# Weight sums by accumulating DMA, moved out of one attention stage and spread over five semaphores

## The chip, the cores and the metric

The kernel runs on one core of a Trainium2 chip. The metric is the device time of one execution in microseconds (us); three runs gave 3639.58 to 3647.89, with a median of 3645.61. The five engines are named as in the profile: PE is TensorE (PEld its weight loads), DVE is VectorE, ACT is ScalarE, POOL is GpSimd, SP is SyncE. Each has its own queue and executes it in order; they meet at semaphores.

## The reference, cut to what matters

The program is two blocks of a network one after the other, all in float32, on 512 tokens of width 1024. The first block has two layers, and only these matter here:

```python
for l in range(2):
    h = rms_norm(x, g_mix[l])
    c_q, c_kv, k_r, qkv_b, qkv_c, gate_logits = split(h @ w_in[l])
    y_a = mla_mixer(c_q, c_kv, k_r, ...)        # latent attention, 8 heads, 4 blocks of 128 queries
    y_b = dilated_mixer(rope(q_b), rope(k_b), v_b)   # 3 groups of 4 heads
    y_c = neighbourhood_mixer(q_c, k_c, v_c, rpb[l]) # 8 heads
    merged = g0 * (y_a @ w_pa[l]) + g1 * (y_b @ w_pb[l]) + g2 * (y_c @ w_pc[l])
    x = x + merged @ w_o[l]
    h = rms_norm(x, g_ffn[l])
    x = x + (silu(h @ w1[l]) * (h @ w3[l])) @ w2[l]
```

The second block (retention, a gated recurrence and two more FFNs) is not touched by the change.

## The kernel before, in words

Every matmul is made of three in single-pass precision: each float32 operand is split into a high and a low part, and high times high, high times low and low times high are added. Weights come from one large DRAM array, `wts`, in chunks of 128 x 1024, in the order in which PE uses them. SP loads chunk after chunk into two slots (`s_raw`); ACT rounds a chunk to its high part (`wh`) and DVE subtracts that for the low part (`wl`). The softmax work stands between these splits in the queues of ACT and DVE by a plan of levels.

Each layer goes through the stages mix (first projections), MLA, dilated attention in two passes (`dil`, p = 0 and 1), neighbourhood attention (`nbr`), the output projection, and the FFN.

- In MLA (`tensor_mla`, `vector_mla`, `scalar_mla`, `gpsimd_mla`) there are 32 steps, one for each head and block of queries. In step i PE transposes the probabilities of step i - 3, makes the scores of step i and fills up with projections; DVE takes the minimum of the negated scores; ACT takes exp with a sum; DVE takes the reciprocal (`vector_div`, L1273); POOL multiplies the 128 x 512 probabilities `m_p` by it (`gpsimd_div`, L713). PE's transposes of step i wait for that product. POOL also turns keys and queries (`b_qk`, `m_ql`).
- A dilated pass has 13 iterations; divisions (`b_p`, 128 x 768) stand in the first 8, projections for later stages fill PE's queue. At the end of pass 0 POOL multiplies six tiles `b_qk`, for which DVE waits in its queue.
- The neighbourhood attention has 21 iterations; the first 16 hold two divisions (`c_p`, 128 x 256) each, and some a gate product (`acc`) or a turned bias (`c_nb`).

The FFN computes most of its tiles (16 of 22 in a layer, the S units) by a scheme of Strassen's kind with seven products, which needs sums of blocks of weights. Four halves a, b, c, d of two neighbouring weight chunks (each 128 x 512) are to give a + b, b + c, a + b + c and a + b + c + d. These sums are made without any engine's arithmetic: POOL issues DMAs from DRAM to DRAM, plain ones and ones that add onto what is there, into the array `sums` (128 x 2048 for each unit). `weight_sums` (L2659) is a generator that issues a little at each `next`; `sum_turn` (L2701) is one turn. A unit takes three plain copies in one turn (512 KB and twice 256 KB), two adds of 256 KB in the next, and an add of 256 KB in each of two later turns, where they share the turn with those of another unit. Every turn first makes POOL wait, on the one semaphore `sa`, until the last DMA of the turn before has landed. A layer has 49 turns with work. `gpsimd_mla` takes one at the end of each of its 41 iterations, so 41 of the 49 are in MLA and 8 in dilated pass 0.

In the FFN, SP loads the sums and the raw halves of a unit (`load_s`, L734) once its last add has landed.

Of the kernel before, what the change touches and what calls it, by code (L numbers as in the profile page):

```python
# [8 lines left out]
ALU = mybir.AluOpType  # L9
# [36 lines left out]
for _j in range(4):  # L46
# [14 lines left out]

    "pw", "sc", "pl",

    "rawf", "raw0", "raw1", "raw2", "raw3", "rawb", "rawh", "sa", "cst0", "cst", "idn", "tab", "rct", "kct", "msk", "cb0", "cb1", "dec", "ret", "out", "out2",
) + tuple(f"xi{i}" for i in range(8))


# [651 lines left out]
class Sp(Line):  # L719
# [13 lines left out]

    def load_s(self, n, slot, side, *unit):  # L734

        m, wts, sums = self.m, self.m.A["wts"], s_sums(self.m, unit)
        f, l, i = unit
        self.wait_ge("sa", "S4", *unit)
        if side == "a":
            self.e.dma_start(m.raw[slot][:, 0:512], wts[n][:, 0:512]).then_inc(*self.tell(f"raw{slot}", "x", n, by=16))  # L740
            self.e.dma_start(m.raw[slot][:, 512:1024], sums[:, 1024:1536]).then_inc(*self.tell(f"raw{slot}", n, by=16))
            return
        self.e.dma_start(m.raw[slot][:, 0:512], wts[n][:, 0:512]).then_inc(*self.tell(f"raw{slot}", "x", n, by=16))
        self.e.dma_start(m.raw[slot][:, 512:1024], sums[:, 1536:2048]).then_inc(*self.tell(f"raw{slot}", n, by=16))
        before = (f, l, i - 1) if KINDS[i - 1] == "S" else (f, 0, FF - 1) if l else None
        if before:
            self.wait_ge("wl", self.book.s_at(0, before))
        else:
            self.wait_ge("mm", "acc", f, l, 0, 0)
        self.e.dma_start(m.s_b, sums[:, 0:1024]).then_inc(*self.tell("rawb", *unit, by=16))  # L750
        if before:
            self.wait_ge("wl", self.book.s_at(2, before))
        self.e.dma_start(m.s_h, wts[n][:, 512:1024]).then_inc(*self.tell("rawh", *unit, by=16))

    def weights(self, upto, least=-1):
        while not self.inside and self.loaded <= self.book.needs(max(upto + 2, least)):
# [206 lines left out]
def gpsimd_b(L, n):  # L963
    _, l, p, g, w = n
    x = L.m.b_qk[p][2 * g + w]
    L.wait_ge("ev", "shift", *n)
    L.wait_ge("ev", "b_tab", l)
    L.tt(x, x, L.m.b_rc, ALU.mult).then_inc(*L.tell("pl", *n))
# [178 lines left out]
def gpsimd_mix(L, l):  # L1147
    m = L.m
    gpsimd_stat(L, ("mix", l))
    L.wait_ge("rv", "q", l)  # L1150
    L.rsqrt(m.qcol, m.vtmp[:, 0:8], 8).then_inc(*L.tell("pw", "q", l))
    gpsimd_q(L, l, 0)
    L.sums = weight_sums(L, l)
# [102 lines left out]
def gpsimd_q(L, l, h):  # L1256
    m = L.m
    L.wait_ge("hi", "q", l, h)
    L.tt(m.m_q[h % 2][1], m.m_qf, b32(m.m_q[h % 2][0]), ALU.subtract).then_inc(*L.tell("pl", "ql", l, h))
# [22 lines left out]
def gpsimd_div(L, i, P, *key):  # L1282
    m, c = L.m, i % 8
    L.wait_ge("rc", *key, i)
    L.ts(P, P, m.rd[:, c:c + 1], 1.0, ALU.mult, ALU.mult).then_inc(*L.tell("sc", *key, i))
# [42 lines left out]
def gpsimd_y(L, yf, hi, lo, i, at, *key):  # L1328
    L.wait_ge("hi", "y", *key, i)
    L.tt(part(lo, at), yf, b32(part(hi, at)), ALU.subtract).then_inc(*L.tell("pl", "y", *key, i))  # L1330
# [144 lines left out]
def gpsimd_mla(L, l):  # L1475
    m = L.m
    for i in range(41):
        if i < 32:
            gpsimd_div(L, i, m.m_p[i % 4], "mla", l)
        if i - 1 in B_TURN:  # L1480
            gpsimd_b(L, ("b", l, 0) + B_TURN[i - 1])
        if i % 4 == 1 and i < 29:
            gpsimd_q(L, l, i // 4 + 1)
        if 14 <= i < 38 and i % 8 == 6:
            gpsimd_y(L, m.m_yf, *m.ya, (i - 14) // 8, (i - 14) // 8, "mla", l)
        sum_turn(L)


def sync_mla(L, l):
# [69 lines left out]
def gpsimd_proj(L, l, br, i):  # L1559
    m = L.m  # L1560
    L.wait_ge("ev", "p", l, br, i)
    L.tt(m.acc[i], m.acc[i], m.g[i % 2], ALU.add).then_inc(*L.tell("pl", "acc", l, br, i))
# [61 lines left out]
def at(p, i, back):  # L1624

    return [(FILL_V if p else FILL_B)[g] for g in ENDS[p][i - back]] if i >= back else []
# [240 lines left out]
def gpsimd_dil(L, l, p):  # L1867
    key = ("dil", l, p)
    for i in range(13):
        if 1 - p <= i < 8:  # L1870
            gpsimd_div(L, i, L.m.b_p[i % 2], *key)
        if p == 0:
            if i == 2:
                gpsimd_y(L, L.m.m_yf, *L.m.ya, 3, 3, "mla", l)
            for n in at(p, i, 2):
                gpsimd_b(L, ("b", l, 1) + n)
        sum_turn(L)


def sync_dil(L, l, p):  # L1880
# [91 lines left out]
def at_n(i, back):  # L1972
    return [FILL_N[g] for g in ENDS_N[i - back]] if i >= back else []
# [154 lines left out]
def gpsimd_bias(L, l, h):  # L2128
    nb = L.m.c_nb[h % 2]
    L.wait_ge(f"cb{h % 2}", "bias", l, h)  # L2130
    L.ts(nb, nb, -1.0, 1.0, ALU.mult, ALU.mult).then_inc(*L.tell("pl", "cb", l, h))


def gpsimd_nbr(L, l):
    key = ("nbr", l)
    gpsimd_bias(L, l, 0)
    gpsimd_bias(L, l, 1)
    for it in range(21):
        if it < 16:
            for i in (2 * it, 2 * it + 1):  # L2140
                gpsimd_div(L, i, L.m.c_p[i % 6], *key)
        if it >= 2 and it % 2 == 0 and it < 14:
            gpsimd_bias(L, l, it // 2 + 1)
        for x, n in at_n(it, 1):
            if x == "p":
                gpsimd_proj(L, l, 1, n)
        sum_turn(L)


# [498 lines left out]
def s_units():  # L2648
    return [i for i in range(FF) if KINDS[i] == "S"]


def s_sums(m, unit):

    f, l, i = unit
    units = s_units()
    return m.A["sums"][len(units) * l + units.index(i)]


def weight_sums(L, l):  # L2659

    book, wts, units = L.book, L.m.A["wts"], s_units()
    last = None

    def add(to, x, *key):
        L.e.dma_start(to, x, accum_op=ALU.add).then_inc(*L.tell("sa", *key, by=16))

    def of(k):
        unit = ("f", l, units[k])
        return (unit, s_sums(L.m, unit)) + tuple(book.ring[book.s_at(0, unit)][3:5])

    for k in range(len(units) + 3):
        if k < len(units):
            unit, s, a, b = of(k)
            if last:
                L.wait_ge("sa", *last)
            L.e.dma_start(s[:, 0:1024], wts[a]).then_inc(*L.tell("sa", "c0", *unit, by=16))
            L.e.dma_start(s[:, 1024:1536], wts[a][:, 0:512]).then_inc(*L.tell("sa", "c1", *unit, by=16))
            L.e.dma_start(s[:, 1536:2048], wts[b][:, 512:1024]).then_inc(*L.tell("sa", "c2", *unit, by=16))
            last = ("c2",) + unit
            yield  # L2680
        if 0 < k <= len(units):
            unit, s, a, b = of(k - 1)
            L.wait_ge("sa", *last)
            add(s[:, 0:512], wts[a][:, 512:1024], "S3", *unit)
            add(s[:, 512:1024], wts[b][:, 0:512], "S1", *unit)
            last = ("S1",) + unit
            yield
        if 1 < k:
            L.wait_ge("sa", *last)
            if k <= len(units) + 1:  # L2690
                unit, s, a, b = of(k - 2)
                add(s[:, 1024:1536], s[:, 512:1024], "S2", *unit)
                last = ("S2",) + unit
            if 2 < k:
                unit, s, a, b = of(k - 3)
                add(s[:, 1536:2048], s[:, 1024:1536], "S4", *unit)
                last = ("S4",) + unit
            yield


def sum_turn(L):  # L2701
    next(L.sums, None)
# [1447 lines left out]
def gpsimd_program(L):  # L4150
    gpsimd_start(L)
    for l in range(2):
        gpsimd_mix(L, l)
        gpsimd_mla(L, l)
        gpsimd_dil(L, l, 0)
        gpsimd_dil(L, l, 1)
        gpsimd_nbr(L, l)
        gpsimd_out(L, l)
        gpsimd_ffn1(L, l)
    gpsimd_ret(L)  # L4160
    gpsimd_ffn2(L, 0)
    gpsimd_lru(L)
    gpsimd_ffn2(L, 1)
# [114 lines left out]
    return np.ascontiguousarray(v.reshape(-1, 128).T)  # L4278


def pack(plan, inputs):
    w = np.zeros((len(plan), 128, 1024), np.float32)
    for c, tiles in enumerate(plan):
        for p, d in enumerate(tiles):
            if d is None:
                continue
            name, lead, row, cols = d
            cols = np.asarray(list(cols))
            blk = inputs[name][lead][row:row + 128]
            real = cols >= 0  # L4290
            w[c, :, 128 * p:128 * p + 128][:, real] = blk[:, cols[real]]
    return w


# [42 lines left out]
```

## Time and profile before

| | |
|---|---|
| median of three runs | 3645.61 us |
| profiled execution | 3644.53 us, of which the span is 3642.3 |
| mean granted clock of PE | 0.946 |
| PE busy | 3311.8 us, 91% |
| DVE, ACT, POOL busy | 1934.1, 1412.6, 775.3 us |
| DMA through POOL's queue (software) | 28160 packets, 67.12 MB, 10.7% of 16 engines |
| DMA through SP's queue (hardware) | 102816 packets, 317.93 MB, 26.6% |
| sum DMAs | 128 adds and 96 copies |

Busy time says how much an engine had to do, not that it had to do it just then. In the slices of the span (91 us each) one sees where PE falls below nine tenths and where its clock (PEclk, tenths of full speed) does. The tables by stage give each engine's busy time between two moments, the granted clock, the mean busy share of the 16 DMA engines and what they moved. The waits name, for each engine, what ended its idle time. A busy time of POOL for a DMA is the time of issuing it, not of the transfer.

### The profile page before, as it was taken

The numbers are of one execution on the slowest core, as the hardware profiler recorded it, in microseconds if no ns is written. First come the engines' busy times: TensorE is split into PE (matmuls) and PEld (weight loads), VectorE is DVE, ScalarE is ACT, GpSimd is POOL, SyncE is SP. The second block draws the span as 40 slices with busy tenths as digits, with TensorE's granted clock in tenths as the row PEclk, the third lists the DMA queues.
The fourth block names the chain that finished last, engine by engine and source line by source line (L and its number), as shares of the span: only waits on it lengthen the run. The fifth ranks groups of instructions, "written<-read, shape, count | busy, mean of one in ns | idle before, by whom it ended". The sixth has DMA issues, their size and how long they took to land. (4 is left out here: it accounts for less than half of the span.)

```text
span 3642.3 us, 41452 instructions
## 1 busy us (share of the span) xinstructions
PE 3311.8 (91%) x16588; PEld 2802.6 (77%) x16588; DVE 1934.1 (53%) x2948; ACT 1412.6 (39%) x2175; POOL 775.3 (21%) x722
## 2 busy tenths in 40 slices
PE   8654799999999655599999999999999999999998
PEld 7443688888898544488888898888888888888887
DVE  5332447567474433256757475655464427885433
ACT  5322335345353322235535353333242225863221
POOL 2432313301010343312311010211021102541101
PEclk9776899999999767799999999999999999999999
DMA  4556513225442556622334353222223222223322
GB/s 159 111 104 117 106 64 112 97 87 161 139 151 98 124 104 125 113 82 100 100 99 141 125 163 107 90 73 95 87 87 102 95 98 87 93 87 99 101 96 81
DMA packets 131744, 388.10 MB, mean 107 GB/s; under 512 B 15200, under 2 KB 17760, under 8 KB 131552
## 3 DMA queue, kind: packets, MB, share of 16 engines
q1 hardware_dynamic: 102816, 317.93, 26.6%
q0 software_dynamic: 28160, 67.12, 10.7%
q8 instruction: 131, 2.15, 0.2%
q14 instruction: 61, 0.50, 0.0%
q10 hardware_dynamic: 576, 0.40, 0.0%
HBM read 383.29 MB, written 69.21 MB: 124 GB/s over the span
## 5 line engine op out<-in xcount | busy, mean ns | idle before, releaser
L352 PE MATMUL bank<-zh,wh 128*128 128x512 f32 (+1 forms) x2588 | 957.4, 370 | 6.0 <-ACT zh L611 6.0
L670 DVE TENSOR_TENSOR wl<-s_raw,wh 128x1024 fp32r<-128x1024 f32 (+1 forms) x531 | 660.3, 1248 | 558.3 <-ACT wh L611 557.2
L352 PE MATMUL bank<-zh,wl 128*128 128x512 f32 (+1 forms) x2588 | 949.4, 367 | 5.6 <-DVE wl L670 5.6
L352 PE MATMUL bank<-zl,wh 128*128 128x512 f32 (+1 forms) x2588 | 948.8, 367 | 2.2 <-DVE zl L673 2.1
L611 ACT ACTIVATE wh<-s_raw 128x1024 fp32r<-128x1024 f32 (+1 forms) x531 | 555.4, 1052 | 479.9 <-PE bank L352 407.6
L352 PEld LDWEIGHTS bank<-zh,wl 128*128 128x128 f32 x2588 | 494.3, 191 | 91.5 <-DVE wl L670 11.8
L352 PEld LDWEIGHTS bank<-zh,wh 128*128 128x128 f32 x2588 | 496.8, 192 | 83.1 <-ACT zh L611 6.0
L352 PEld LDWEIGHTS bank<-zl,wh 128*128 128x128 f32 x2588 | 495.6, 191 | 78.6 <-DVE zl L673 3.7
L710 POOL TENSOR_TENSOR f_t<-f_t 128x512 f32<-128x512 f32 x84 | 119.3, 1421 | 880.6 <-DVE f_t L666 880.6
L355 PE MATMUL bank<-ident,m_p 128*128 128x128 f32 x256 | 55.9, 358 | 178.6 <-POOL m_p L713 175.6
L716 POOL TENSOR_TENSOR small<-small 128x1 f32<-128x1 f32 (+3 forms) x35 | 43.0, 1230 | 821.9 <-DVE small L663 821.9
L355 PEld LDWEIGHTS bank<-ident,m_p 128*128 128x128 f32 x256 | 37.0, 181 | 206.0 <-issue 195.5
L1448 DVE TENSOR_REDUCE small<-bank 128x1 f32<-128x512 f32 x64 | 44.1, 689 | 212.3 <-PE bank L352 212.1
L352 PE MATMUL bank<-wh,zh 128*128 128x512 f32 (+2 forms) x384 | 147.0, 383 | 0.0
L352 PE MATMUL bank<-f_mh,wh 128*128 128x512 f32 (+1 forms) x396 | 146.4, 370 | 0.0
L352 PE MATMUL bank<-wh,zl 128*128 128x512 f32 (+2 forms) x384 | 145.6, 379 | 0.0
L352 PE MATMUL bank<-f_mh,wl 128*128 128x512 f32 (+1 forms) x396 | 145.3, 367 | 0.0
L352 PE MATMUL bank<-wl,zh 128*128 128x512 f32 (+2 forms) x384 | 145.3, 378 | 0.0
L352 PE MATMUL bank<-f_ml,wh 128*128 128x512 f32 (+1 forms) x396 | 144.2, 364 | 0.0
L352 PE MATMUL bank<-h_h,wl 128*128 128x512 f32 x352 | 138.7, 394 | 0.0
L352 PE MATMUL bank<-h_l,wh 128*128 128x512 f32 x352 | 138.0, 392 | 0.0
L352 PE MATMUL bank<-h_h,wh 128*128 128x512 f32 x352 | 136.6, 388 | 0.0
(383 smaller groups left out, 6169.3 us busy)
## 6 DMA issues: line engine op xcount, KB each, us to landing
s_raw<-in_wts SPq DMA_DIRECT2D x465, 512.0 KB, 3.3
sums<-in_wts POOLq DMA_DIRECT2D x128, 256.0 KB, 5.3
s_raw<-in_wts SPq DMA_DIRECT2D x66, 256.0 KB, 3.0
sums<-in_wts POOLq DMA_DIRECT2D x32, 512.0 KB, 4.6
sums<-sums POOLq DMA_DIRECT2D x64, 256.0 KB, 5.6
s_raw<-sums SPq DMA_DIRECT2D x64, 256.0 KB, 3.8
s_b<-sums SPq DMA_DIRECT2D x32, 512.0 KB, 3.8
s_h<-in_wts SPq DMA_DIRECT2D x32, 256.0 KB, 2.6
```

The source lines that it names most:

```text
L352: return self.e.matmul(out, l, r, start=start, stop=stop, skip_group_check=inside)
L355: return self.e.transpose(out, in_, self.m.ident)
L611: return self.e.activation(out, in_, ACT.Copy, scale=scale)
L670: return self.e.tensor_tensor(out, src, b32(hi), ALU.subtract)
L710: return self.e.tensor_tensor(out, a, b, op)
L716: return self.e.tensor_tensor(out, v, self.m.negh[:, 0:n], ALU.pow)
L1448: L.e.tensor_reduce(m.mn[:, c:c + 1], m.bank[4 + i % 2], AX.X, ALU.min).then_inc(*L.tell("mn", "mla", l, i))
```

## The change

The order in which the DRAM holds the weights of an S unit changes: the two chunks of a unit are laid side by side, so that a row of 2048 elements (a, b, c, d) is one piece of 8 KB (`pack`, `s_raw_tiles`). `load_s` takes its halves from there. A unit is now one plain copy of 1 MB, one add of 512 KB that makes a + b and b + c together, and two adds of 256 KB: four DMAs, each alone in a turn. The turns run through five semaphores, `sa0` to `sa4`, and each waits only for the last DMA on its own, which is the fifth turn back. `gpsimd_mla` has no `sum_turn` any more; each iteration of the dilated passes and of the neighbourhood attention has two. A layer takes 76 turns (64 with a DMA): 52 in the dilated passes and 24 in the first 12 iterations of the neighbourhood attention.

```diff
@@ load_s @@
-        self.wait_ge("sa", "S4", *unit)
+        self.wait_ge(sums_done(i), "S4", *unit)
+        x, y = (0, 1024) if side == "a" else (1024, 1536)
+        self.e.dma_start(m.raw[slot][:, 0:512], raw[:, x:x + 512])...
+        self.e.dma_start(m.raw[slot][:, 512:1024], sums[:, y:y + 512])...
...
@@ gpsimd_mla @@
-        sum_turn(L)
@@ gpsimd_dil @@
         sum_turn(L)
+        sum_turn(L)
@@ gpsimd_nbr @@
         sum_turn(L)
+        sum_turn(L)
@@ weight_sums @@
+def s_raw_tiles(m, n):
+    return m.A["wts"][n:n + 2].rearrange("c p x -> (c p x)").rearrange("(p x) -> p x", x=2048)
...
+    def dma(turn, to, x, *key, **kw):
+        sem = f"sa{turn % 5}"
+        if sem in last:
+            L.wait_ge(sem, *last[sem])
+        L.e.dma_start(to, x, **kw).then_inc(*L.tell(sem, *key, by=16))
+        last[sem] = key
...
     for k in range(len(units) + 3):
...
+        if k < len(units):
+            unit, s, raw = of(k)
+            dma(4 * k, s, raw, "copy", *unit)
+        yield
+        if 0 <= k - 1 < len(units):
+            unit, s, raw = of(k - 1)
+            dma(4 * k + 1, s[:, 0:1024], raw[:, 512:1536], "S31", *unit, accum_op=ALU.add)
+        yield
+        if 0 <= k - 2 < len(units):
+            unit, s, raw = of(k - 2)
+            dma(4 * k + 2, s[:, 1024:1536], s[:, 0:512], "S2", *unit, accum_op=ALU.add)
+        yield
+        if 0 <= k - 3:
+            unit, s, raw = of(k - 3)
+            dma(4 * k + 3, s[:, 1536:2048], s[:, 1024:1536], "S4", *unit, accum_op=ALU.add)
+        yield
+def sums_done(i):
+    return f"sa{(4 * (s_units().index(i) + 3) + 3) % 5}"
@@ pack @@
+    for c in pairs:
+        w[c:c + 2] = np.concatenate([w[c], w[c + 1]], axis=1).reshape(2, 128, 1024)
```

## Rows read from the trace of the kernel before

**Rows 1.** Page, slices: busy tenths of PE and its clock.

```profile
PE   8654799999999655599999999999999999999998
PEclk9776899999999767799999999999999999999999
```

**Rows 2.** By stage: length; busy (x instructions) of each engine; clock, DMA share, GB/s.

```profile
66.90:290.80 223.90, 135.53 (x501) 106.14 (x499) 77.12 (x145) 66.26 (x130) 92.70 (x120) 0.74 0.58 112
290.80:483.10 192.30, 125.41 (x589) 104.06 (x590) 70.81 (x132) 52.51 (x89) 48.41 (x55) 0.80 0.55 111
483.10:577.40 94.30, 93.53 (x470) 77.06 (x469) 48.75 (x90) 37.06 (x62) 12.54 (x10) 1.00 0.25 81
577.40:640.90 63.50, 63.50 (x338) 53.68 (x337) 57.66 (x125) 43.57 (x91) 31.46 (x31) 1.00 0.31 106
1191.90:1418.00 226.10, 134.66 (x501) 104.51 (x499) 77.02 (x145) 66.59 (x130) 92.89 (x120) 0.73 0.57 111
1418.00:1598.80 180.80, 124.91 (x589) 104.65 (x590) 69.73 (x132) 52.52 (x89) 50.21 (x56) 0.80 0.57 118
```

**Rows 3.** Waits of PE and POOL, whole span: total us, times, longest.

```profile
PE bank L355 <- POOL m_p L713: 175.6, 59, 6.1
PE bank L355 <- POOL b_p L713: 86.1, 7, 39.7
...
POOL m_p L713 <- DVE small L1273: 19.0, 2, 9.7
```

**Rows 4.** POOL in order of time: start, us, engine, line, operation [idle before].

```profile
66.89 0.71 POOL L713 TENSOR_SCALAR m_p<-m_p,small 128x512 f32<-128x512 f32 x1 [9.30 <-DVE small L1273]
...
203.09 1.74 POOL L2665 DMA_DIRECT2D sums<-in_wts  x2 [5.17 <-DMA sums<-in_wts]
204.25 1.31 POOL L713 TENSOR_SCALAR m_p<-m_p,small 128x512 f32<-128x512 f32 x1
...
290.78 0.72 POOL L713 TENSOR_SCALAR m_p<-m_p,small 128x512 f32<-128x512 f32 x1
```

**Rows 5.** DVE in order of time, one MLA step.

```profile
217.22 0.69 DVE L1448 TENSOR_REDUCE small<-bank 128x1 f32<-128x512 f32 x1 [7.41 <-PE bank L352]
...
218.76 0.16 DVE L1273 RECIPROCAL small<-small 128x1 f32<-128x1 f32 x1 [0.25 <-ACT m_p L614]
```

**Rows 6.** By window: a copy alone, then two adds alone, at work.

```profile
340.00:342.00 2.00, 0.00 (x0) 0.00 (x0) 0.00 (x0) 0.00 (x0) 0.00 (x0) 1.00 1.05 301
346.00:348.00 2.00, 0.00 (x0) 0.00 (x0) 0.00 (x0) 0.00 (x0) 0.00 (x0) 0.50 1.02 100
```

**Rows 7.** POOL in order of time: issues of sums.

```profile
295.53 1.74 POOL L2665 DMA_DIRECT2D sums<-in_wts  x2 [4.03 <-DMA sums<-in_wts]
306.12 1.66 POOL L2665 DMA_DIRECT2D sums<-sums  x2 [8.85 <-DMA sums<-in_wts]
...
337.99 0.54 POOL L2676 DMA_DIRECT2D sums<-in_wts  x1 [5.22 <-DMA sums<-sums]
...
344.02 1.70 POOL L2665 DMA_DIRECT2D sums<-in_wts  x2 [4.40 <-DMA sums<-in_wts]
352.66 1.64 POOL L2665 DMA_DIRECT2D sums<-sums  x2 [6.94 <-DMA sums<-in_wts]
...
1232.59 0.84 POOL L2665 DMA_DIRECT2D sums<-sums  x1 [5.74 <-DMA sums<-in_wts]
...
1237.87 0.57 POOL L2676 DMA_DIRECT2D sums<-in_wts  x1 [3.70 <-DMA sums<-sums]
```

**Rows 8.** The FFN by window, and SP's loads of sums: first and last start.

```profile
831.00:1140.00 309.00, 309.00 (x1994) 282.32 (x1995) 190.71 (x283) 139.74 (x197) 24.31 (x18) 1.00 0.45 143
...
L741 SPq DMA_DIRECT2D s_raw<-sums x32: 432/432/1482, 831.2 to 2161.2; - x32
```

**Rows 9.** POOL in order of time: divisions of neighbourhood iterations 0 and 11.

```profile
577.45 0.98 POOL L713 TENSOR_SCALAR c_p<-c_p,small 128x256 f32<-128x256 f32 x2 [25.81 <-DVE small L1273]
...
640.90 1.89 POOL L713 TENSOR_SCALAR c_p<-c_p,small 128x256 f32<-128x256 f32 x2 [1.02 <-DVE small L1273]
```

More of the change, by code:

```diff
@@ L62 @@
     "pw", "sc", "pl",
-    "rawf", "raw0", "raw1", "raw2", "raw3", "rawb", "rawh", "sa", "cst0", "cst", "idn", "tab", "rct", "kct", "msk", "cb0", "cb1", "dec", "ret", "out", "out2",
+    "rawf", "raw0", "raw1", "raw2", "raw3", "rawb", "rawh", "sa0", "sa1", "sa2", "sa3", "sa4", "cst0", "cst", "idn", "tab", "rct", "kct", "msk", "cb0", "cb1", "dec", "ret", "out", "out2",
 ) + tuple(f"xi{i}" for i in range(8))
@@ L734, in load_s @@
     def load_s(self, n, slot, side, *unit):
-        m, wts, sums = self.m, self.m.A["wts"], s_sums(self.m, unit)
+        m, sums = self.m, s_sums(self.m, unit)
+        raw = s_raw_tiles(m, n if side == "a" else n - 1)
         f, l, i = unit
-        self.wait_ge("sa", "S4", *unit)
+        self.wait_ge(sums_done(i), "S4", *unit)
+        x, y = (0, 1024) if side == "a" else (1024, 1536)
+        self.e.dma_start(m.raw[slot][:, 0:512], raw[:, x:x + 512]).then_inc(*self.tell(f"raw{slot}", "x", n, by=16))
+        self.e.dma_start(m.raw[slot][:, 512:1024], sums[:, y:y + 512]).then_inc(*self.tell(f"raw{slot}", n, by=16))
         if side == "a":
-            self.e.dma_start(m.raw[slot][:, 0:512], wts[n][:, 0:512]).then_inc(*self.tell(f"raw{slot}", "x", n, by=16))
-            self.e.dma_start(m.raw[slot][:, 512:1024], sums[:, 1024:1536]).then_inc(*self.tell(f"raw{slot}", n, by=16))
             return
-        self.e.dma_start(m.raw[slot][:, 0:512], wts[n][:, 0:512]).then_inc(*self.tell(f"raw{slot}", "x", n, by=16))
-        self.e.dma_start(m.raw[slot][:, 512:1024], sums[:, 1536:2048]).then_inc(*self.tell(f"raw{slot}", n, by=16))
         before = (f, l, i - 1) if KINDS[i - 1] == "S" else (f, 0, FF - 1) if l else None
@@ L752, in load_s @@
             self.wait_ge("wl", self.book.s_at(2, before))
-        self.e.dma_start(m.s_h, wts[n][:, 512:1024]).then_inc(*self.tell("rawh", *unit, by=16))
+        self.e.dma_start(m.s_h, raw[:, 1536:2048]).then_inc(*self.tell("rawh", *unit, by=16))
     def weights(self, upto, least=-1):
@@ L2656, in s_sums @@
     return m.A["sums"][len(units) * l + units.index(i)]
+def s_raw_tiles(m, n):
+    return m.A["wts"][n:n + 2].rearrange("c p x -> (c p x)").rearrange("(p x) -> p x", x=2048)
 def weight_sums(L, l):
[L2661 to L2665, printed above, removed]
+    book, units = L.book, s_units()
+    last = {}
+    def dma(turn, to, x, *key, **kw):
[4 more added lines that the diff above has]
+        last[sem] = key
@@ L2667, in of @@
     def of(k):
         unit = ("f", l, units[k])
-        return (unit, s_sums(L.m, unit)) + tuple(book.ring[book.s_at(0, unit)][3:5])
+        return unit, s_sums(L.m, unit), s_raw_tiles(L.m, book.ring[book.s_at(0, unit)][3])
     for k in range(len(units) + 3):
         if k < len(units):
[L2673 to L2698, printed above, removed]
+            unit, s, raw = of(k)
@@ L4278, in columns, with pack @@
     return np.ascontiguousarray(v.reshape(-1, 128).T)
-def pack(plan, inputs):
+def pack(plan, pairs, inputs):
     w = np.zeros((len(plan), 128, 1024), np.float32)
@@ L4332 @@
     arrays = {f"in_{n}": v for n, v in d.items()}
-    arrays["in_wts"] = pack(book.plan, a)
+    arrays["in_wts"] = pack(book.plan, sorted({r[3] for r in book.ring if r[0] == "s"}), a)
     r = _run(nc, [arrays], core_ids=[0])
```

## Prediction

> **What bounds the kernel now.** I read the slices of the page first [rows 1]. TensorE (PE) is busy nine tenths and at its full clock nearly everywhere, but in slices 2 to 5 and 14 to 17 it is busy four to seven tenths and its granted clock falls as well. The same stretch comes twice, so it is one stage of each of the two layers. The table by stage [rows 2] gives it edges: latent attention (MLA) from its first to its last division on GpSimd (66.9 to 290.8 and 1191.9 to 1418.0), and from there to the first division of the second dilated pass (290.8 to 483.1 and 1418.0 to 1598.8). PE is busy 135.5 of 223.9 us and 125.4 of 192.3 us, at clocks 0.74 and 0.80. Behind that, in dilated pass 1 and the neighbourhood attention, it is busy 99% or more at 1.00.
>
> The waits say who is late [rows 3]: PE's transposes waited 175.6 us for GpSimd's division of m_p (59 of 64 times) and 86.1 us for that of b_p, while GpSimd waited for its own input of m_p twice. GpSimd's queue is the bound, and not by its arithmetic. Its timeline shows why [rows 4]: each division (about 1 us) stands behind a turn of the weight sums, and each turn starts with idling until the last sum DMA has landed (5.17 us before the one at 203.09, 4.03 before that at 295.53 [rows 7]). 31 steps take 223.9 us, 7.2 us each. The whole kernel's time is thus lost in two places of 416 and 407 us, and the rest doesn't hang on the sums.
>
> **The change part by part.** All against the profiled execution, 3644.5 us (span 3642.3 and 2 us around it); the median of the runs is 1.1 us above it.
>
> *The turn leaves MLA.* 41 turns with their waits and issues go. What is late next? VectorE's step is a chain [rows 5]: the minimum starts at 217.22, then exp on ScalarE, and the reciprocal starts at 218.76 and ends 0.16 later: 1.70 us, of which VectorE idles 0.25 just before the reciprocal. With its 77.1 us of work in 31 steps [rows 2], 2.49 each, and that 0.25, VectorE's step is 2.7 us. ScalarE has 66.3 / 31 = 2.1. PE has 501 matmuls; where it runs without gaps it needs 94.3 / 470 = 0.20 us for each in pass 1 and 63.5 / 338 = 0.19 in the neighbourhood stage [rows 2], so 94 to 100 us, 3.0 to 3.2 us a step, if its clock is full. Three engines that near to each other cost some waiting: I take 3.3 us, 102 us in all. The ends are 2.7 (VectorE's alone) and 6.5 (PE at half its clock: 501 at 0.40). The gain is 223.9 - 102 = 122 and 226.1 - 102 = 124 us.
>
> On the clock: rows 2 show 0.74, between the levels of 1.2 and 2.4 GHz, where PE idles 88 of 224 us, and 1.00 where it does not. The Trainium skill ("TensorE: Matmul & The Clock Gate", Part 1) says the same of the cause: throttled is the default, and activity releases it. It speaks for the full clock once the gaps are gone.
>
> *Eight turns leave the head of dilated pass 0.* There GpSimd, with nothing else to do, works off turn after turn while PE waits for its first b_p: one wait of 39.7 us is in the 86.1. From 290.8 to 483.1 PE has 589 matmuls, 118 us at 0.20. The start of the pass has a chain of its own (turned keys, their low parts, first scores), for which I add 12 us: 130. The gain is 62 and 51 us. The ends: 118 (nothing is exposed), and 160 if half of the present idle time has other causes.
>
> *Two turns in each iteration of the dilated passes and the neighbourhood attention.* 76 turns a layer, 64 of which issue a DMA: 52 in pass 0 and pass 1, 24 in the first 12 iterations of the neighbourhood attention. The bytes are the same 2.1 MB a unit, in 4 DMAs in place of 7. GpSimd's own part: an accumulate occupies it 0.87 us (1.74 for two [rows 4]), a copy about 0.54 [rows 7], so some 3.2 us for two iterations. In the neighbourhood attention GpSimd is busy 31.5 of 63.5 us [rows 2]; 1.6 us on an iteration of 5.8 makes 77%. That alone hides.
>
> The wait for the fifth one back does not stall on latency: it reaches 2.5 iterations back, 14 us at least, and a DMA alone needs 5.3 us from its issue to the next turn [rows 7]. What counts is how much the 16 DMA engines can take. Here two rows speak [rows 6]: a plain copy fills them (share 1.05) and moves 301 GB/s; an accumulate fills them as well (1.02) and moves 100 GB/s. A unit is 1.05 MB copied, 3.5 us, and 1.05 MB accumulated, 10.5 us: 14.0 us of all engines, 3.5 us a turn. The weight loads come on top.
> - Pass 0: 26 turns, 91 us, and about 15 us of weights, in 130 us. Hidden.
> - Pass 1 (94.3 us): 26 turns, 91 us, and 81 GB/s of weights, 7.6 MB at 301 GB/s, 25 us: 116, or 22 too many. Five DMAs in flight lend 17. 5 us are left.
> - Neighbourhood attention, iterations 0 to 11 (first division 577.45, last 640.90, 5.8 us each [rows 9]): 7.0 us of sums and 106 GB/s of weights, 0.61 MB, 2.0 us: 9.0 us. 3.2 us too many, twelve times: 39 us.
> What waits behind a held turn on GpSimd is the next two divisions, the gate products and the turned bias, then PE's transposes, and VectorE, which waits for b_k and the bias in order. PE then has gaps again, and I add 6 us for its clock. Cost: 50 us a layer, 100 in all. Below it could be 0, if accumulates of different units overlap better than two of one unit do; above 75, if engines are only nine tenths full in practice.
>
> That row decides against a rule of the Trainium skill. "DMA: Bandwidth & Descriptors", Anatomy of one DMA, fits a GpSimd DMA as 2.0 us and its bytes at 436 GB/s; an estimate by that page is 4.8 us of movement for a unit in place of 14.0, and then the cost would be nothing and the time 3286. The trace disagrees for accumulates, at 100 GB/s.
>
> *The layout of the pairs, the merged adds, the new addresses in the loads.* Rows of 8 KB in place of 4 KB; the loads of the sum units still take 2 KB a row. They lie beside an FFN in which PE is busy 309.0 of 309 us at 1.00 [rows 8], and are hidden. Landing half a microsecond later would cost nothing there. The sums end in iteration 11 of the neighbourhood attention, some 190 us before the first load of them at 831 [rows 8]: nothing there becomes late. At the worst 5 us.
>
> Sum: 3644.5 - (122 + 124) - (62 + 51) + 100 = 3385.5, about 3386 us.
>
> **The rivals.**
> A. *The DMA engines don't bind.* The cost of 100 is not there: 3286 us. For it: the two rows are of one or two DMAs at a time. Against it: their share is full already.
> B. *MLA's next chain is slower.* PE, VectorE and ScalarE wait for each other, PE's gaps keep its clock between the levels, and a step takes 4.8 us, 149 in all: 94 us less gained, 3480. For it: three loads between 2.1 and 3.2 us with work of 1.2 us in one piece among them. Against it: in the neighbourhood attention VectorE is busy 57.7 of 63.5 us and PE still has no gap [rows 2].
> C. *The turns come one after the other, so slower than before.* If five semaphores buy no overlap, because accumulates get in each other's and the weight loads' way, a unit costs what it costs now: a copy 6.0 us (337.99 to 344.02), the joined add 8.6 (344.02 to 352.66), the two short ones 5.3 each (1232.59 to 1237.87) [rows 7], 25.2 us. Beside weight loads the add took 10.6 (295.53 to 306.12); the whole unit scaled by that is 31 us. 16 units then need 496 us, where pass 0, pass 1 and 12 iterations give 130 + 94 + 64 = 288: 208 us lost a layer, against 180 won. 3644.5 - 359 + 416 = 3702 us. It turns slower above 29.2 us a unit. Against it: nothing in the order holds a turn but the fifth one back.
> D. *A heavier form of my cost*, 75 to 90 us a layer, weights late too: 3435 to 3470.
>
> **How the numbers follow.** My forecast 0.50 (3330 to 3435), A 0.21, B 0.12, D 0.11, C 0.04, and 0.02 for something else that takes all the gain. The range 3295 to 3485 leaves out A's lower end, C and B's upper end. A measurement of this kernel tells 0.2% (7 us) from no change. All cases but C and the last are faster: 0.95; same 0.01; slower 0.04.
>
> **What would show it.** Right: in MLA the steps of m_p about 3.3 us apart, PE's wait for m_p gone to a few us, the clock near 1.00 there; the first wait of PE in pass 0 under 10 us; DMA share near 1 in the neighbourhood attention, GpSimd idle before its sums there on a DMA, and its twelve iterations 8 to 9 us apart in place of 5.8. If these stay at 5.8, A holds; steps of 4.5 us and more in MLA are B; turns 6 to 8 us apart all through are C. The forecast is wrong as a whole if MLA stays near 7 us a step without any sum in it.

## The result, and the profile after

The changed kernel takes 3319.7 us (median of 4 runs, 3317.6 to 3326.3), the kernel before in the same session 3644.3: a ratio of 0.911, 95% interval 0.910 to 0.913. It is 325 us faster; the forecast was 3386, 259 us faster, with 3295 to 3485 as its range. The profiled execution took 3321.6 us, its span 3319.8.

Of the page of the kernel after, the slices (busy tenths of PE, its clock, the DMA engines' share). The two holes in PE's row and in its clock [rows 1] are gone; what is left are eights in slices 5, 6, 16 and 17, where the DMA row shows six to nine:

```profile
PE   9999889999999998899999999999999999999998
PEclk9999989999999999899999999999999999999999
DMA  3176862254431379742345422222232322223232
```

By stage, the kernel after, cut at the same divisions as [rows 2]: length; busy (x instructions) of PE, PEld, DVE, ACT, POOL; clock, DMA share, GB/s:

```profile
67.00:149.30 82.30, 80.81 (x458) 67.52 (x456) 71.02 (x139) 59.95 (x126) 49.73 (x46) 1.00 0.14 46
149.30:284.50 135.20, 124.78 (x632) 104.29 (x633) 73.54 (x138) 55.11 (x94) 37.46 (x38) 0.96 0.62 158
284.50:392.90 108.40, 96.80 (x470) 78.49 (x469) 48.45 (x90) 37.31 (x62) 31.90 (x37) 0.94 0.85 191
392.90:473.10 80.20, 68.46 (x330) 56.18 (x330) 56.82 (x125) 43.49 (x91) 44.70 (x47) 0.89 0.80 182
...
1025.30:1107.60 82.30, 80.86 (x458) 67.48 (x456) 71.02 (x139) 59.96 (x126) 49.74 (x46) 1.00 0.14 45
1107.60:1240.70 133.10, 124.96 (x632) 104.72 (x633) 73.70 (x138) 55.23 (x94) 37.40 (x38) 0.96 0.65 161
1240.70:1347.50 106.80, 96.89 (x469) 78.82 (x469) 48.48 (x90) 37.19 (x62) 31.91 (x37) 0.95 0.85 194
1347.50:1431.10 83.60, 69.46 (x338) 56.51 (x337) 58.10 (x125) 43.45 (x91) 43.70 (x48) 0.92 0.78 175
```

| us, layer 0 / layer 1 | before | forecast | after |
|---|---|---|---|
| MLA | 223.9 / 226.1 | 102 | 82.3 / 82.3 |
| dilated pass 0 | 192.3 / 180.8 | 130 | 135.2 / 133.1 |
| dilated pass 1 | 94.3 / 94.3 | 99 | 108.4 / 106.8 |
| neighbourhood, iterations 0 to 11 | 63.5 / 63.5 | 102 | 80.2 / 83.6 |
| PE's clock | | 6 | in the rows |

MLA and pass 0 give 390 us in both layers together, pass 1 and the first 12 neighbourhood iterations take back 63. PE's waits over the whole span, kernel after (total us, times, longest). GpSimd's m_p and b_p [rows 3] are no longer among them; in their place stand ScalarE's high part of the weights (wh), VectorE's low part (wl) and the low part of c_p:

```profile
PE bank L352 <- ACT wh L611: 31.6, 8, 9.9
PE bank L352 <- DVE wl L670: 17.3, 17, 4.9
PE bank L355 <- DVE c_ptl L670: 12.6, 6, 3.1
```

Why ScalarE is late is to be seen one step further back, in the waits of ScalarE and GpSimd themselves from 149 to 475 us (layer 0), and in one place of the timeline. The waits:

```profile
ACT wh L611 <- DMA s_raw<-in_wts: 66.7, 12, 13.9
...
POOL sums L2674 <- DMA sums<-in_wts: 19.5, 7, 4.2
POOL sums L2674 <- DMA sums<-sums: 10.9, 7, 2.9
```

Rows from 424 to 444 us, in the neighbourhood attention (start, us, engine, line, operation [idle before <- releaser]; here each engine's rows one after the other, first GpSimd's, then SP's queue, then ScalarE):

```profile
425.76 1.41 POOL L2674 DMA_DIRECT2D sums<-in_wts  x2
...
430.29 1.67 POOL L2674 DMA_DIRECT2D sums<-sums  x2
443.04 1.89 POOL L713 TENSOR_SCALAR c_p<-c_p,small 128x256 f32<-128x256 f32 x2 [11.07 <-DVE small L1273]
...
426.31 2.08 SPq L732 DMA_DIRECT2D s_raw<-in_wts  x2
...
441.19 1.06 ACT L611 ACTIVATE wh<-s_raw 128x1024 fp32r<-128x1024 f32 x1 [11.92 <-DMA s_raw<-in_wts]
```

SP issues a weight load at 426.31, between four sum DMAs of GpSimd. ScalarE then stands idle 11.9 us until a weight load has landed (the two issued here took 16.2 us in the median), VectorE and PE behind it, and GpSimd's next division, 11 us later, is held by their work and not by its sums. GpSimd waited only 30 us for sum DMAs in the whole stretch. So the cost of the change is there, but on another road than forecast: not GpSimd held at its turns, but weight loads made late. Its size is measured below (e9).

### The profile page after: what moved, and what is told of

Its sections match the earlier page's. It is cut to its first block, busy times and chain, and to the rows that moved or that the text cites. A ratio compares the mean times of both kernels' runs of the same rounds, so it can differ in the third digit from the quotient of the medians.

```text
span 3319.8 us, 41356 instructions
## 1 busy us (share of the span) xinstructions
PE 3224.9 (97%) x16588; PEld 2739.3 (83%) x16588; DVE 1928.6 (58%) x2948; ACT 1404.8 (42%) x2175; POOL 730.9 (22%) x626
## 3 DMA queue, kind: packets, MB, share of 16 engines
q0 software_dynamic: 14848, 67.12, 10.4%
## 4 chain that ended last, share of the span: by engine, by line
PE 78%; DVE 8%; DMA 6%; ACT 4%; issue 2%; POOL 2%; SPq 0%; ACTq 0%; DVEq 0%; POOLq 0%
PE bank L352 76%; DMA s_raw<-in_wts 5%; DVE wl L670 2%; PE bank L355 2%; ACT wh L611 1%; ACT m_p L614 1%; DVE small L1448 1%; DMA sums<-in_wts 1%; POOL f_t L710 1%; POOL u_g L710 1%; DVE c_kl L670 1%; DVE u_uc L666 0%; DVE m_ptl L670 0%; DVE b_k0l L670 0%; DVE m_qf L660 0%
## 5 line engine op out<-in xcount | busy, mean ns | idle before, releaser
L352 PE MATMUL bank<-zh,wl 128*128 128x512 f32 (+1 forms) x2588 | 949.7, 367 | 15.8 <-DVE wl L670 15.7
L352 PE MATMUL bank<-n_h,wh 128*128 128x256 f32 (+1 forms) x448 | 133.7, 298 | 2.2 <-ACT wh L611 2.2
L352 PE MATMUL bank<-n_h,wl 128*128 128x256 f32 (+1 forms) x448 | 133.2, 297 | 0.9 <-DVE wl L670 0.9
L352 PE MATMUL bank<-n_l,wh 128*128 128x256 f32 (+1 forms) x448 | 133.1, 297 | 0.0
## 6 DMA issues: line engine op xcount, KB each, us to landing
s_raw<-in_wts SPq DMA_DIRECT2D x66, 256.0 KB, 3.1
sums<-sums POOLq DMA_DIRECT2D x64, 256.0 KB, 10.8
s_raw<-sums SPq DMA_DIRECT2D x64, 256.0 KB, 3.7
s_h<-in_wts SPq DMA_DIRECT2D x32, 256.0 KB, 2.6
```

Of the source, the lines that this page charges most:

```text
L352: return self.e.matmul(out, l, r, start=start, stop=stop, skip_group_check=inside)
```

## The experiments

Twelve kernels ran. All times are medians, each with its ratio to the kernel before on the same chip. The stages of layer 0, cut at the same divisions (in the row of e1 and e9 those of e9):

| | us | MLA | pass 0 | pass 1 | nbr. 0 to 11 |
|---|---|---|---|---|---|
| before | 3644 | 223.9 | 192.4 | 94.3 | 63.4 |
| after | 3319.7 | 82.4 | 135.2 | 108.4 | 80.2 |
| e1, e9: no sums | (3499), 3218.8 | 82.4 | 119.4 | 94.3 | 63.0 |
| e11: one row of each sum | 3227.4 | 82.3 | 118.8 | 94.3 | 62.8 |
| e8: plain copies | 3286.3 | 82.4 | 129.8 | 104.0 | 72.9 |
| e7: third one back | 3316.0 | 82.3 | 135.3 | 106.3 | 78.0 |
| e2: last one | 3510.0 | 82.4 | 172.3 | 150.6 | 100.1 |
| e4: old DMAs, new place | 3583.8 | 82.4 | 216.2 | 183.1 | 62.2 |
| e5: new DMAs, old place, last one | 3460.4 | 147.4 | 165.8 | 96.4 | 67.2 |
| e3: new DMAs, old place, fifth one | 3279.9 | 85.5 | 132.2 | 101.3 | 69.2 |
| e6: spread | 3269.0 | 82.4 | 127.6 | 102.3 | 70.4 |
| e12: spread, third one back | 3272.1 | 82.4 | 127.6 | 101.6 | 70.3 |
| e13: spread, more in MLA | 3276.9 | 82.5 | 125.4 | 101.4 | 73.3 |

### What the sums cost: e1, e9, e11, e8

**e1.** The turns do nothing, and the loads of the sum units take the raw weights:

```diff
 def sum_turn(L):
+    return
     next(L.sums, None)
```

> This kernel leaves the weight sums out: no turn issues a DMA and the loads of the S units take raw halves, so its output is not the reference's. It measures what the sums still cost where they now stand. Theory (the sums share the 16 DMA engines with the weight loads, and late loads stop ACT, VectorE and PE): pass 1 falls from 108 to 94 us, the first 12 neighbourhood iterations from 80 to 63.5 us, pass 0 from 135 to about 125 us; in both layers together some 80 us, so 3240 us, and ACT's waits of 6 to 14 us for s_raw go. Rival (the sums are hidden and those waits have another cause): 3300 to 3320 us with the waits still there.

Measured: 3499.1 us (0.959). Both missed, by a slip of mine: the FFN's start on GpSimd still runs the generator to its end, so all 64 sum DMAs of a layer were issued there one behind the other, and PE waited 273.8 us for GpSimd behind them (3 waits, longest 137.9). Its stages before that point are those without sums. The heap at the FFN's start is a measurement of its own: the DMA engines by window, kernel e1, while nothing but sums runs:

```profile
600.00:660.00 60.00, 0.00 (x0) 0.00 (x0) 0.00 (x0) 0.00 (x0) 14.83 (x20) 0.50 1.06 194
```

Full engines (1.06) move 194 GB/s of mixed copies and adds: a unit of 2.1 MB takes 2.1 / 194 = 10.8 us of all 16, not the 14.0 of the forecast.

**e9.** The same, with the generator empty:

```diff
-    for k in range(len(units) + 3):
+    for k in ():
```

> The changed kernel without any sum DMA, also none at the start of the FFN; the loads take the halves of the weights as they are, so the output is not the reference's. Theory (the sums take 47 us a layer in dilated pass 0, pass 1 and the neighbourhood attention, and nothing elsewhere): 3319.7 - 94 = about 3226 us, 3215 to 3240; the stages as in the first run without sums: pass 0 about 119, pass 1 94, neighbourhood iterations 0 to 11 64 us. Rival (the stages lengthened for another reason, or the loads behind are slowed too): above 3250, or below 3210 if the sums also cost something beyond iteration 11.

Measured: 3218.8 us (0.884 [0.883, 0.885]), in the theory's range. The changed kernel is 3319.7 - 3218.8 = 101 us longer, where the forecast had 100 for the sums. Its first three stages behind MLA, to be laid beside those of after:

```profile
149.30:268.80 119.50, 118.95 (x632) 101.61 (x633) 73.73 (x138) 55.34 (x94) 23.47 (x18) 1.00 0.23 76
268.80:363.10 94.30, 93.54 (x470) 77.06 (x469) 48.69 (x90) 37.14 (x63) 12.57 (x11) 1.00 0.24 81
363.10:426.10 63.00, 63.00 (x334) 53.32 (x333) 57.05 (x125) 43.63 (x91) 32.04 (x31) 1.00 0.31 108
```

PE has no gap here, with the clock at 1.00. The differences, 15.7, 14.1 and 17.2 us in layer 0 (14.3, 12.6 and 21.0 in layer 1), make 95 us. The remaining 6 lie outside these stages, and 4.7 of them are not the sums': from the start of PE's last matmul to the end it is 12.3 us in the kernel after, 12.4 in the kernel before and 7.6 in e9. So the sums cost some 96 us. The 95 are gaps and clock: PE's busy time for the same (in the last stage nearly the same) matmuls rose from 118.95 to 124.78, from 93.54 to 96.80 and from 63.0 to 68.5 us, 14.6 of the 47 us of layer 0.

**e11.** Every issue and every wait as they are, but one row of 128 moved:

```diff
-        L.e.dma_start(to, x, **kw)
+        L.e.dma_start(to[0:1], x[0:1], **kw)
```

> The changed kernel with all 64 sum DMAs a layer issued in their places and waited for as they are, but each moves one row of 128 only, and the loads of the sum units take the weights as they are, so the output is not the reference's. Theory (what costs is the time that the sums take of the DMA engines, here under 1% of it): 3219 to 3230 us, as without any sums. Rival (GpSimd's issue of a DMA, some 0.5 to 0.9 us each, or its waits, cost the third that plain copies left over): 3250 to 3290.

Measured: 3227.4 us (0.887 [0.886, 0.888]), the theory. The stages are those without sums to 0.6 us; the 8.6 us above e9 lie after 1335 us, behind the sums of both layers, and 7.8 of them behind the start of PE's last matmul (15.4 us to the end, against 7.6 in e9); why the kernel's end differs between runs is not known. So GpSimd's 64 issues cost nothing in the stages: the bytes do. The waits are not tested by e11, where GpSimd was never idle before a sum DMA; in the changed kernel it waited 30 us for them from 149 to 475 us, and none of PE's waits there names one of its divisions.

**e8.** The same bytes, waits and places, but nothing is added:

```diff
-            dma(4 * k + 1, s[:, 0:1024], raw[:, 512:1536], "S31", *unit, accum_op=ALU.add)
+            dma(4 * k + 1, s[:, 0:1024], raw[:, 512:1536], "S31", *unit)
```

and so for the other two adds.

> The same four DMAs a unit in the same places with the same waits and bytes, but the three adds are plain copies, so the sums are not the reference's. Theory 1 (what makes the weight loads late is the engine time of accumulates, 100 GB/s against 301 for a copy): a unit then takes about 7 us of all engines in place of 14, and most of the 47 us a layer goes: 3235 to 3270 us, waits of ScalarE for its weights under 7 us. Theory 2 (the number of GpSimd's DMAs and their issue cost it, whatever they do): about as the changed kernel, 3305 to 3325.

Measured: 3286.3 us (0.902 [0.901, 0.904]), between the two: 67.5 of the 101 us stay. GpSimd's queue in the page (packets, MB, share of 16 engines), of the kernel after:

```profile
q0 software_dynamic: 14848, 67.12, 10.4%
```

and of e8:

```profile
q0 software_dynamic: 10752, 67.12, 6.5%
```

10.4% of 3319.8 us over 32 units is 10.8 us a unit, as the heap of e1 has it; 6.5% of 3284.5 is 6.7. The engine time falls to 0.62 of what it was, and the cost in the three stages behind MLA to 0.63 (30.0 and 29.7 us a layer in place of 47.0 and 47.9). Theory 1 had the engine time right, with 7 us a unit, but wrongly took a plain copy's share to be nearly free.

### Depth: e2, e7

**e2** has one semaphore, so that each turn waits for the last sum DMA. **e7** has three, and each turn waits for the last DMA issued three or more turns back. Nothing else changes. The edit of e2 in the turns (`sums_done` follows):

```diff
-        sem = f"sa{turn % 5}"
+        sem = f"sa{turn % 1}"
```

> The changed kernel with one semaphore: the same DMAs in the same places, but each turn waits for the one before it. Theory (the five semaphores carry a part of the gain: a unit in series costs 25 to 31 us, 400 to 496 us for 16, in a window of some 320 us): GpSimd is late again in pass 1 and in the neighbourhood attention, 80 to 180 us more a layer, 3480 to 3680 us. Rival (the place alone is worth it, and fewer DMAs in flight even spare the weight loads): 3290 to 3340 us.

> The changed kernel with its places, but each sum DMA waits for the third one back in place of the fifth. Theory 1 (weight loads are late because sums of several units are in flight with them: fewer in flight, shorter lateness; GpSimd waits more but has slack): 3295 to 3315 us. Theory 2 (only the engine time of the sums counts, which is the same): 3315 to 3325. Rival (three are not enough for two turns in each iteration; GpSimd is held and PE waits for b_p and c_p as with one): 3340 to 3430.

Measured: with the last one 3510.0 us (0.962 [0.961, 0.963]), in the theory's range; with the third one back 3316.0 (0.911 [0.910, 0.912]), in the range of theory 2 and 1 us from that of theory 1, with runs on both sides of their border, so that the time alone doesn't choose. GpSimd's waits for its sums over the whole span, kernel e2:

```profile
POOL sums L2674 <- DMA sums<-in_wts: 303.0, 57, 9.0
POOL sums L2674 <- DMA sums<-sums: 224.4, 61, 6.9
```

527 us of waiting, and now the turns do hold the divisions (PE waits 51.3 us for c_p and 43.4 for b_p): this is where rival C lives. The three stages behind MLA take 423 us for 16 units, 26.4 each, under the 29.2 from which C would have been slower than before, and e2 is faster than before. With three, the time is that of five (3.7 us apart, intervals that overlap), though the sums land sooner. Median landing from 149 to 475 us (issues, KB each, us; the line without a size is the plain copies), kernel after:

```profile
s_raw<-in_wts SPq DMA_DIRECT2D x39, 512.0 KB, 5.1
sums<-in_wts POOLq DMA_DIRECT2D x16, 512.0 KB, 10.1
sums<-sums POOLq DMA_DIRECT2D x32, 256.0 KB, 10.5
sums<-in_wts POOLq DMA_DIRECT2D x16, 6.9
```

kernel e7:

```profile
s_raw<-in_wts SPq DMA_DIRECT2D x40, 512.0 KB, 5.4
sums<-in_wts POOLq DMA_DIRECT2D x16, 512.0 KB, 9.5
sums<-sums POOLq DMA_DIRECT2D x32, 256.0 KB, 8.5
sums<-in_wts POOLq DMA_DIRECT2D x16, 6.8
```

kernel e9, up to 430 us:

```profile
s_raw<-in_wts SPq DMA_DIRECT2D x39, 512.0 KB, 3.3
```

In the median a weight load lands in 5.1 us beside sums and in 3.3 without; in e7 it is no sooner (5.4), and in e2, with one sum in flight, neither (5.4, from 149 to 573 us). The median hides the tail: taken load by load from the traces, the longest lands after 27.1 us in the kernel after, 23.2 in e7, 8.6 in e2 and 7.0 in e9. And e7 changed little: counts times landings over 326 us make 1.9 sum DMAs in flight on average after the change and 1.6 in e7 (an estimate from the rows above). So e7 does not bear out my theory that the number in flight makes loads late, but does not exclude it either.

Where the late ones are the DMA engines are full. Their busy tenths in 40 slices from 149 to 475 us (8.15 us each), kernel after:

```profile
DMA  0731186989899840388988999899337949993976
```

and the window of ScalarE's wait in the timeline above (in the order of the table by stage; PE busy 10.33 of 15 us, DMA share 1.01):

```profile
428.00:443.00 15.00, 10.33 (x56) 8.50 (x54) 4.12 (x12) 2.92 (x6) 3.67 (x4) 0.91 1.01 236
```

Pass 0 has a mean share of 0.62, but slices 8 to 14 of this row (206 to 263 us) stand at eight and nine tenths, and ScalarE's long waits of that pass (7.7 us before 241.0, 13.9 before 256.0) lie there. Load by load, each of the 9 that took over 9 us found the engines 0.94 to 1.06 busy while it was on its way.

### Place and DMAs: e4, e5, e3

**e4**, the kernel before with its turns moved:

```diff
 (MLA)
-        sum_turn(L)
 (dilated, neighbourhood)
         sum_turn(L)
+        sum_turn(L)
```

> The kernel before with nothing changed but the place: its seven DMAs a unit, its one semaphore and its waits for the last DMA, but no turn in MLA and two in each iteration of the dilated passes and the neighbourhood attention. Theory (the place brings the gain of MLA, 141 us a layer, and without the five semaphores most of it is lost again: 49 turns of 7 to 8 us, 15 us an iteration where 7.5 are needed, +100 to +130 us a layer in the dilated passes): 3520 to 3600 us. Rival (the place alone makes the gain): 3320 to 3360 us.

**e5**, the changed kernel with the turns at their old places and the wait for the last one; **e3**, the same with the five semaphores kept:

```diff
 (MLA)
+        sum_turn(L)
 (dilated, neighbourhood)
         sum_turn(L)
-        sum_turn(L)
```

> The new layout and the new four DMAs a unit, but the old places (one turn in each iteration of MLA, of the dilated passes and of the neighbourhood attention) and each DMA waiting for the one before. Theory (the old wait for the last DMA is what costs; fewer DMAs make 64 waits of 112): MLA's 41 turns stay held, PE waits for GpSimd's m_p and b_p: 3560 to 3660 us. Rival (the merged DMAs alone bring the gain, since a unit costs less in all): 3400 to 3500.

> The changed kernel with the turns where they were before (one at the end of every iteration of MLA, of the dilated passes and of the neighbourhood attention), but with the new DMAs and five semaphores. Theory (what hurt MLA was the wait for the last DMA; the engines bear about 3.5 us a turn): 41 turns need some 140 us of DMA in an MLA of 110 us, so MLA is 115 to 150 us in place of 82, and later stages get back 15 to 25 us: 3340 to 3420 us. Rival (any turn in MLA is as bad as before, since the division stands behind it): MLA stays near 200 us a layer, 3530 us or more.

Measured: e4 3583.8 us (0.982 [0.981, 0.984]), e5 3460.4 (0.950 [0.948, 0.951]), e3 3279.9 (0.899 [0.897, 0.900]). e4 came as the theory had it, the other two against it: e5 in the rival's range, e3 faster than the change itself. Put together:

| us | old place | new place |
|---|---|---|
| 7 DMAs, wait for the last | 3644 | 3584 |
| 4 DMAs, wait for the last | 3460 | 3510 |
| 4 DMAs, wait for the fifth back | 3280 | 3320 |

Fewer and larger DMAs, one in a turn, are worth 184 us at the old place and 74 at the new, five semaphores 180 to 190 at either. The 184 hold more than the DMAs' own cost: with one DMA in a turn MLA holds 25 of a layer's 64 in e5 and e3, where the kernel before had 73 of its 112 there. The old DMAs with the wait for the fifth back were not run. The move is worth 60 with the old DMAs (MLA's 141.5 us, of which pass 0 and pass 1 take back 112.6) and *costs* 40 to 50 with the new ones. In e3 GpSimd issues all through MLA and waits only 4.9 us for sum DMAs there; its stage, kernel e3:

```profile
66.60:152.10 85.50, 83.52 (x476) 69.64 (x475) 72.11 (x140) 61.28 (x128) 65.33 (x72) 1.00 0.94 201
```

The DMA engines are 0.94 full, and MLA is 3.1 us longer than without sums (5.4 in layer 1): it has few weight loads, 46 GB/s against 76 to 108 in the stages behind it. Its 6 loads are late too (8.1 us in the median, 3.2 in e9), but ScalarE does not wait for one of them.

### Spread: e6, e12, e13

**e6**: e3 with the turn in every other iteration of MLA, and one after each of the 8 steps of the output projection:

```diff
 (MLA)
+        if i % 2:
+            sum_turn(L)
 (output projection)
         gpsimd_proj(L, l, 2, i)
+        sum_turn(L)
```

**e12** is e6 with the wait for the third one back, **e13** e6 with `i % 3` for `i % 2`.

> Five semaphores, one turn in each iteration of the dilated passes and the neighbourhood attention, one in every other iteration of MLA, and 8 in the output projection. Theory (what costs is how many sum DMAs are in flight at once beside weight loads; fewer turns in an iteration make fewer): at or below the run with one turn in every iteration of MLA (3280): 3260 to 3285 us. Rival (the turns moved out of MLA into the neighbourhood attention and the output projection hit weight loads there, where DMAs are already busy, and MLA has room): 3290 to 3320.

> One turn in every other iteration of MLA, one in each of the dilated passes and the neighbourhood attention, 8 in the output projection (3269 with the fifth one back), here with the third one back. Theory: at this pace at most one or two sums are in flight, the wait hardly ever binds, and the time is the same: 3260 to 3275 us. Rival (bursts of turns in the short iterations are what makes loads late, and three in flight cut them): 3245 to 3260. If three hold GpSimd: above 3280.

> As the run with one turn in every other iteration of MLA, but in two of three there (27 turns in place of 20), fifth one back. Theory: MLA's DMA engines have room (weights take 0.14 of them), so its stage stays near 82 us and each turn taken out of the later stages gives back about 47 us / 64 = 0.7 us: 2 x 7 x 0.7 = 10 us less, about 3259, 3255 to 3265. Rival (in MLA each turn costs what it costs later, as the run with one in every iteration, 85.5 to 87.8 us there, suggests): 3266 to 3276.

Measured: 3269.0 us (0.898 [0.897, 0.899]), 3272.1 (0.899 [0.897, 0.900]) and 3276.9 (0.901 [0.899, 0.902]). e6 and e12 came in the ranges of their theories, e13 on its rival's side. For e6 that does not show its theory: its range begins 20 us under the time of e3 and ends above it, and the number in flight is what e7 left open. By stage, MLA first, kernel e6:

```profile
66.70:149.10 82.40, 80.87 (x458) 67.61 (x456) 71.08 (x139) 59.98 (x126) 55.32 (x55) 1.00 0.48 121
149.10:276.70 127.60, 122.88 (x632) 104.56 (x633) 73.66 (x138) 55.33 (x94) 36.23 (x35) 0.96 0.61 148
276.70:379.00 102.30, 96.90 (x470) 78.76 (x469) 48.59 (x90) 37.17 (x62) 21.94 (x23) 0.97 0.56 141
379.00:449.40 70.40, 65.52 (x339) 54.94 (x338) 57.26 (x125) 43.59 (x91) 38.64 (x41) 0.98 0.62 163
```

ScalarE's wait for weight loads from 149 to 475 us, kernel e6, against 66.7 us after:

```profile
ACT wh L611 <- DMA s_raw<-in_wts: 32.5, 10, 8.3
```

The turns in MLA are free here (82.4 us, share 0.48), and with one turn in an iteration the other stages pay half: 8.2, 8.0 and 7.4 us above e9, with 18, 13 and 11 sum DMAs in them where the kernel after has 20, 26 and 17. Pass 0 pays half with nearly as many, so their number in a stage is not the whole cost; that they come less closely together is the likely reason, which no run shows by itself.

e13 should have gained by more turns in MLA and lost 8. Its premise was wrong: the turns that went to MLA (14 sum DMAs there in place of 9) came from behind the neighbourhood iterations (6 left of 13), and pass 1 and the neighbourhood iterations kept their 13 and 11. So there was nothing to gain in those two. MLA is as long, the neighbourhood iterations are 2 to 3 us longer, and pass 0 is 2.2 us shorter in layer 0 and 2.7 longer in layer 1; why, is open. e6, 51 us faster than the change, has the lowest time of all, with e12 within the noise of it.

## Why the prediction was right, and where it was not

**The bound, read right.** GpSimd's turns held MLA and pass 0. Without them PE's waits for m_p and b_p are gone and the clock of MLA went from 0.74 to 1.00. The Trainium skill ("TensorE: Matmul & The Clock Gate", Part 1) takes activity for what releases the throttle; the trace agrees, 80.8 of 82.3 us busy at 1.00.

**MLA: the term that was mis-sized.** Forecast 3.3 us a step, 102; measured 82.3, 2.66 a step, in both layers. That is 39 of the 66 us by which the forecast was too high (22 more are the start of pass 0, below). The step that failed is PE's work: I took all 501 matmuls of the old window at 0.20 us, the time of stages with wider ones (236 of the 501 have fewer than 384 columns, in pass 1 140 of 470). The new window holds 458 (43 had only been drawn into it by the delays, and stand in pass 0 now: 632 for 589), and they take 80.8 us, 0.176 each. I added 0.1 to 0.3 us a step for engines near to each other, and there was hardly any: PE idles 1.5 us in 31 steps. The step even came in under the lower end of 2.7, which was VectorE's: the new window holds 71.0 us of its work and not 77.1. Rival B (4.8 us a step) was far off.

**Pass 0: right for a wrong reason.** Forecast 130, measured 135.2 and 133.1. Its floor is 118.8 to 119.4 as I took it (118), but the 12 us for its start are not there (PE idles 0.5 us in e9), and the sums, which I called hidden, cost 14 to 16.

**The cost of the sums: size right by luck, road wrong.** Forecast 100 in all, measured 96 to 101. Errors of both signs met. Too high: a unit takes 10.8 us of the engines and not 14.0. The 100 GB/s of [rows 6] are a window of 2 us and not typical; the page of the kernel before already had 10.7% of 3642.3 us for 32 units, 12.2 each. It is not a matter of how many are in flight: e2 and e5, with one at a time, have 9.7% of 3508.6 us and 9.8% of 3461.4, 10.6 a unit. Too high as well: I charged 3.5 us for each of the 24 turns in the neighbourhood iterations, of which 18 hold a DMA, 21 us of my 39 there. They are 7.3 us apart (80.2 / 11) and not 8 to 9, with a DMA share of 0.80, and lost 17.2 and 21.0 us.

Too low: I set the mean share of a whole stage against the engines' limit, and let nothing cost before that is reached. But at a mean of 0.62, in pass 0, they are full for stretches (the slices under e7), where single loads land late and stop ScalarE, VectorE and PE. So pass 1 lost 14.1 and 12.6 us where I had 5, pass 0 what is said above, and the slower clock, which is in these numbers, was 15 in layer 0 where I had 6 a layer. I had foreseen GpSimd idle before its sums; from 149 to 475 us it waits 30 us for them while ScalarE waits 67 for loads.

**Rival A** (no cost, 3286) fell with e9. The estimate by the Trainium skill for it ("DMA: Bandwidth & Descriptors", Anatomy of one DMA), 4.8 us of movement a unit, is short of both measurements: 6.7 for plain copies (e8) and 10.8 with adds. **C** needs the turns to come one after the other; e2 shows what that would have been, 3510 us (26.4 us a unit, where C had 31), and five semaphores prevent it. **D** was right in that weights are late, wrong in its size.

**What the prediction did not see.** It priced the change as moving the turns out of MLA, and counted 246 us for it. That gain is real for the old turns (e4: MLA at 82.4 us), but it did not need the move. With the turns left in MLA, one DMA in each brings the stage from 223.9 to 147.4 us (e5), and the wait for the fifth back in place of the last to 85.5 (e3). With both, turns in MLA cost 3 to 5 us, and moving them into stages with more weight loads costs 40.

## What to carry to other kernels

When an instruction that waits stands in a busy queue, price the removal of the wait apart from the removal of the instruction: here, with one DMA in a turn, the first was worth 180 us and the second less than nothing. Put background DMAs where the latency-bound loads are few, not where the issuing engine is idle, and thinly. Do not compare a stage's mean share of the DMA engines with full engines: look for the stretches inside it where they are full, and count the cost in late loads and in the clock of the engine that they stop. Here a wait for the third transfer back was as good as one for the fifth, and one for the last was not. Take a rate from a whole run's page, not from a window of 2 us.

## What the runs showed of the hardware that was not expected

- An accumulating DMA and a plain one of the same bytes in this kernel: 10.8 against 6.7 us of all 16 engines for a unit of which half is added. If both plain halves cost the same, the added half costs 2.2 times the copied one ((10.8 - 3.35) / 3.35, an estimate), less than the threefold of [rows 6]. With one in flight at a time (e2, e5) it is 10.6 us, so several in flight neither save nor cost engine time.
- With sums in the background the median weight load lands in 5.1 us in place of 3.3, and single ones keep ScalarE idle for 12 to 14 us. One sum in flight leaves the median as it is (5.4), but the longest load is 8.6 us in place of 27.1.
- PE's granted clock fell to 0.89 in the neighbourhood stage with gaps of 11.7 of 80.2 us, and a third of what the sums cost in layer 0 was this slower work, not the gaps.
